# Sparse experts in fp32: from one expert at a time with split weights to four at once in four column tiles of TensorE

## What is computed

```python
lg = xt @ w_rg + b_rg;  g_sel = argmax(lg)                       # one of 4 groups
le = logits of the 8 experts of that group;  e_loc = top 2
gates = p_group * softmax(le_top)
hid = silu(xb @ w_gate[e]) * (xb @ w_up[e])                      # [rows, 512]
y   = hid @ w_down[e]                                            # [rows, 1024]
out[token] += gate * y
```

## Time and profile before

| | |
|---|---|
| median of three runs | 1968.96 us (1967.96 to 1968.97) |
| the profiled execution's own time | 1966.37 us |
| its span, first to last instruction | 1964.6 us |
| mean granted TensorE clock | 0.979 |
| busy: TensorE, its weight loads, VectorE, ScalarE | 94%, 82%, 69%, 56% |
| read from HBM | 406.22 MB, 207 GB/s over the span |
| expert units | 129 of 1536 KB |

### The profile page before, as it was taken

The page is one execution under the profiler, slowest core; times in us unless marked ns, Lnnn a source line. Parts: engine busy times, 40 slices in busy tenths (PEclk is TensorE's granted clock), DMA queues, the critical chain, the costliest instruction groups (busy, mean ns, idle before and its releaser), DMA issues.

```text
span 1964.6 us, 29402 instructions
## 1 busy us (share of the span) xinstructions
PE 1854.7 (94%) x11922; PEld 1601.3 (82%) x11922; DVE 1354.3 (69%) x1835; ACT 1093.9 (56%) x1613; POOL 10.2 (1%) x12
## 2 busy tenths in 40 slices
PE   7998899999999998999999989998899978899997
PEld 5887677777777776999888889998899967799996
DVE  3625999999999996665533376555778785266564
ACT  3234888888988895444323354445644362344444
POOL 0000000000000000000000000000000020000000
PEclk9999999999999999999999999999899988999999
DMA  6325899999999994544244354543498411554420
GB/s 254 119 80 219 308 362 360 358 374 359 362 369 353 364 369 178 210 178 165 88 138 131 113 216 177 185 171 129 166 116 266 140 45 45 182 195 179 182 105 22
DMA packets 56476, 409.30 MB, mean 208 GB/s; under 512 B 15360, under 2 KB 20992, under 8 KB 22160
## 3 DMA queue, kind: packets, MB, share of 16 engines
q1 hardware_dynamic: 51792, 400.51, 57.0%
q10 hardware_dynamic: 4544, 6.85, 1.2%
HBM read 406.22 MB, written 1.11 MB: 207 GB/s over the span
## 4 chain that ended last, share of the span: by engine, by line
PE 67%; DVE 28%; ACT 3%; issue 1%; DMA 0%; DVEq 0%; ACTq 0%; SPq 0%
PE wk L1595 25%; DVE ws_moe L1069 16%; PE acc L1573 11%; PE wk L378 5%; PE wk L1023 3%; PE wk L1948 3%; PE wk L384 2%; PE wk L1763 2%; PE wk L947 2%; PE acc L913 2%; PE acc L730 1%; DVE rstd L305 1%; PE acc L1977 1%; DVE sq L1136 1%; DVE xp_moe L1091 1%
## 5 line engine op out<-in xcount | busy, mean ns | idle before, releaser
L1069 DVE TENSOR_TENSOR ws_moe<-ring,ws_moe 128x1024 fp32r<-128x1024 f32 x384 | 447.5, 1214 | 5.6 <-ACT ws_moe L1062 5.4
L1062 ACT ACTIVATE ws_moe<-ring 128x1024 fp32r<-128x1024 f32 x384 | 384.3, 1051 | 5.1 <-PE wk L1023 2.2
L1595 PE MATMUL wk<-hx,gu 128*128 128x256 f32 x2112 | 276.5, 289 | 5.3 <-DVE hx L1623 4.5
L1595 PEld LDWEIGHTS wk<-hx,gu 128*128 128x128 f32 x2112 | 267.6, 195 | 14.1 <-DVE hx L1623 6.7
L1023 PE MATMUL wk<-ws_moe,xp_moe 128*128 128x512 f32 x1024 | 269.9, 406 | 1.6 <-DVE xp_moe L1091 1.6
L1595 PEld LDWEIGHTS wk<-hx,gu_ffn 128*128 128x128 f32 x2112 | 259.0, 192 | 3.1
L1595 PE MATMUL wk<-hx,gu_ffn 128*128 128x256 f32 x2112 | 260.3, 283 | 0.0
L1573 PE MATMUL acc<-dn_ffn,hh_ffn 128*128 128x512 f32 x1056 | 255.5, 391 | 0.0
L1539 ACT ACTIVATE hT<-hT 128x256 f32<-128x256 f32 x88 | 36.8, 418 | 349.8 <-DVE hT L1642 349.8
L1023 PEld LDWEIGHTS wk<-ws_moe,xp_moe 128*128 128x128 f32 x1024 | 187.9, 189 | 44.2 <-issue 2.8
L1573 PEld LDWEIGHTS acc<-dn_ffn,hh_ffn 128*128 128x128 f32 x1056 | 192.9, 188 | 36.8
(11 more groups left out here) (368 smaller groups left out, 2337.7 us busy)
## 6 DMA issues: line engine op xcount, KB each, us to landing
ring<-in_u_moe SPq DMA_DIRECT2D x129, 1536.0 KB, 8.5
ring<-in_u_ffn SPq DMA_DIRECT2D x88, 1536.0 KB, 6.2
ring<-in_u_qkv SPq DMA_DIRECT2D x12, 1024.0 KB, 5.1
ring<-in_u_ple SPq DMA_DIRECT2D x8, 1280.0 KB, 5.5
ring<-in_u_in SPq DMA_DIRECT2D x9, 1024.0 KB, 5.0
ring<-in_u_glu SPq DMA_DIRECT2D x8, 1024.0 KB, 5.0
ring<-in_u_out SPq DMA_DIRECT2D x4, 1024.0 KB, 4.9
ring<-in_u_o SPq DMA_DIRECT2D x4, 1024.0 KB, 5.1
```

What stands on the lines that cost most here:

```text
L1062: e.activation(WS[:, n % NWS, 0, :], piece(x), ACT.Copy).then_inc(s.m_hi, 1)
L1069: e.tensor_tensor(WS[:, n % NWS, 1, :], piece(x), WS[:, n % NWS, 0, :].bitcast(F32), SUB).then_inc(s.m_lo, 1)
L1595: m = e.matmul(b[:, a * T:(a + 1) * T], gu_of(c, f)[:, x, a * 1024 + k * 128:a * 1024 + (k + 1) * 128], HX[:, y, k, :], start=k == 0 and a ...
```

## The change

- `CAP` goes from 64 to 32 and the experts are worked four at a time (`EPG` = 4, `NG` = 8 groups). Each of the four has its own 32 of the 128 columns of TensorE: its 32 gathered tokens are the stationary operand (128 x 32), its weights stream past in 512 columns, and its result goes to partitions 32x to 32x + 31 of the same PSUM bank.
- The weights are taken in plain fp32 from where they landed. `split_hi`, `split_lo`, `WS`, `tail`, `fold_pe`, `hid_hi`, `hid_lo`, `y_tail` and `y_add` are gone. An expert is no longer worked in halves.
- The DMA units are laid out anew, 128 of 1536 KB, a group being 16 units of three 128 x 1024 pieces; the four experts' pieces of the same rows stand next to each other. They go through eleven slots: six new ones (`ext`) in the space that the split weights had, and the five of `ring`. A slot is free when TensorE has used its third piece (`m_used`).
- The first six units go to `ext` when the mixer's scratch is no longer used (`acc_full` of its last products), the next five when the mixer's last units in `ring` are gone.
- Gather, gates and combine are done once per group of four, 8 times rather than 16.

The core of the diff (places that change with it in the fallback and the host's layout are left out):

```diff
@@ -17,11 +17,12 @@
 NSLOT = 5
-NWS = 8
+NXS = 6
 SCR = 25900
 UNIT = 3072
 NEXP = 32
-CAP = 64
+CAP = 32
+EPG = 4
...
+NG = NEXP // EPG
+NPIECE = 12 * EPG
+NM = NEXP * 12 // 3
+NMS = NXS + NSLOT
...
-        scr2, WS, Xp, MH, gtail, shift, scr2b = area(
...
+        scr2, ext = area("_moe", ("scr", [128, 8192], F32), ("ext", [128, NXS, UNIT], F32))
...
+        def piece_in(e, g, P):
+
+            m = g * NPIECE // 3 + P // 3
+            if P % 3 == 0:
+                e.wait_ge(m_landed[m % NMS], 16 * (m // NMS + 1))
+            return berth_of(m)[:, P % 3 * 1024:P % 3 * 1024 + 1024]
+
+        def moe_sp(e):
+            for m in range(NM):
+                if m < NXS:
+                    e.wait_ge(s.acc_full, fulls("gla") + 1)
+                elif m < NMS:
+                    for w in gone[moe_at - NSLOT + m - NXS]:
+                        e.wait_ge(*w)
+                else:
+                    e.wait_ge(s.m_used, m - NMS + 1)
+                e.dma_start(berth_of(m), A["u_moe"][m]).then_inc(m_landed[m % NMS], 16)
...
+        def gate_up_pe(e, g, k):
+            w = [piece_in(e, g, EPG * k + x) for x in range(EPG)]
+            for a in range(2):
+                for x in range(EPG):
+                    m = e.matmul(wkt[a][slots(x), :], XG[g % 2][:, k, slots(x)], w[x][:, a * 512:a * 512 + 512], start=k == 0, stop=k == 7)
+                    if a and (EPG * k + x) % 3 == 2:
+                        m.then_inc(s.m_used, 1)
+            if k == 7:
+                m.then_inc(s.m_gu, 1)
...
+        def down_pe(e, g):
+            e.wait_ge(s.m_hid, g + 1)
+            e.wait_ge(s.m_G, g + 1)
+            if g + 1 < NG:
+                e.wait_ge(s.m_xa, g + 2)
+                e.wait_ge(s.m_xb, g + 2)
+            for t in range(4):
+                w = [piece_in(e, g, EPG * (8 + t) + x) for x in range(EPG)]
                 for hf in range(2):
-                    for z in range(2):
-                        m = e.matmul(wkt[2 + hf][:, :], MH[:, u % 2, t, :], w[:, z, hf * 512:(hf + 1) * 512],
-                                     start=u % 2 == 0 and t == 0 and z == 0, stop=u % 2 == 1 and t == 1 and z == 1, skip_group_check=True)
-                m.then_inc(s.m_used, 1)
+                    for x in range(EPG):
+                        m = e.matmul(wkt[2 + hf][slots(x), :], mhid[:, t * 128 + CAP * x:t * 128 + CAP * x + CAP], w[x][:, hf * 512:hf * 512 + 512],
+                                     start=t == 0, stop=t == 3)
+                        if hf and (EPG * (8 + t) + x) % 3 == 2:
+                            m.then_inc(s.m_used, 1)
...
+            for g in range(NG):
+                for k in range(8):
+                    gate_up_pe(e, g, k)
+                    if k == 1 and g:
+                        combine_pe(e, g - 1)
+                    if k == 2:
+                        gates_pe(e, g)
+                    if k == 3 and g + 1 < NG:
+                        gather_pe(e, g + 1, 0, wkt[3])
+                    if k == 5 and g + 1 < NG:
+                        e.wait_ge(s.m_G, g + 1)
+                        gather_pe(e, g + 1, 1, wkt[2])
+                hid_pe(e, g)
+                down_pe(e, g)
+            combine_pe(e, NG - 1)
...
         def moe_act(e):
-            split_hi(e, *parts[0:3])
...
+            for g in range(NG):
+                if g + 1 < NG:
+                    gather_act(e, g + 1, wkt[3])
+                e.wait_ge(s.m_gu, g + 1)
+                e.activation(msil, wkt[0][:, :], ACT.Silu).then_inc(s.m_sil, 1)
+                e.wait_ge(s.m_tr, g + 1)
+                e.activation(mhid, wkt[0][:, :], ACT.Copy).then_inc(s.m_hid, 1)
+                e.wait_ge(s.m_used, NPIECE // 3 * (g + 1))
+                if g >= 2:
+                    e.wait_ge(s.m_comb, g - 1)
+                e.activation(ysm[g % 2][:, 512:1024], wkt[3][:, :], ACT.Copy).then_inc(s.m_yl, 1)
...
+                if moe_at <= n < moe_at + NSLOT:
+
+                    e.wait_ge(s.m_used, max(m for m in range(NM) if m % NMS == NXS + (i - moe_at) % NSLOT) + 1)
+                elif n >= NSLOT:
```

More of the change, by code:

```diff
@@ L203, in program @@
         landed = [sem(f"landed{i}") for i in range(NSLOT)]
-        b_landed = [sem(f"b_landed{i}") for i in range(NSLOT)]
+        m_landed = [sem(f"m_landed{i}") for i in range(NMS)]
         ld_bt = [sem(f"ld_bt{i}") for i in range(2)]
@@ L843, in program @@
         rc = S2.get(2)
-        Sel = [S2.get(2, 2, 64) for _ in range(2)]
+        Sel = [S2.get(2, EPG, CAP) for _ in range(2)]
         SG = [S2.get(2, 128) for _ in range(2)]
-        GT_ = [S2b.get(T) for _ in range(2)]
+        XG = [S2.get(8, 128) for _ in range(2)]
+        msil = S2.get(512)
+        mhid = S2.get(512)
+        norms.then("ffn")
+        GT_ = [rstd[:, 1 - norms("ffn") % 2, x * T:(x + 1) * T] for x in range(2)]
         ysm = [sq[:, 4 * x:4 * x + 4, :].rearrange("p a t -> p (a t)") for x in range(2)]
-        msil = [S2b.get(T) for _ in range(2)]
         gm, goh, gex, gsum = R[:, :, 0:1], R[:, :, 1:5], R[:, :, 5:9], R[:, :, 9:10]
@@ L859, in program, with berth_of, gather_pe @@
         first_banks = [i for i in range(4) if i != rank_bank][1:]
[L864 to L894, removed]
+        moe_at = len(units)
+        def berth_of(m):
+            i = m % NMS
+            return ext[:, i, :] if i < NXS else ring[:, (i - NXS + moe_at) % NSLOT, :]
+        def piece_in(e, g, P):
[13 more added lines that the diff above has]
+                e.dma_start(berth_of(m), A["u_moe"][m]).then_inc(m_landed[m % NMS], 16)
+        def gather_pe(e, g, hf, b):
+            e.wait_ge(s.sel, g + 1)
             for k in range(4):
@@ L905, in gates_pe @@
             m.then_inc(s.m_gt, 1)
[L907 to L934, removed]
-            m.then_inc(s.m_tr, 1)
@@ L937, in down_pe, with combine_pe @@
-        def down_pe(e, u):
-            e.wait_ge(s.m_mhl, u + 1)
-            if u % 2 == 0 and u:
-                e.wait_ge(s.m_y, u)
-            for t in range(2):
-                x = (u + 1, 4 + t)
-                e.wait_ge(*split_of(x))
-                w = WS[:, part_at[x] % NWS, :, :]
-                for hf in range(2):
-                    for z in range(2):
-                        m = e.matmul(wkt[2 + hf][:, :], MH[:, u % 2, t, :], w[:, z, hf * 512:(hf + 1) * 512],
-                                     start=u % 2 == 0 and t == 0 and z == 0, stop=u % 2 == 1 and t == 1 and z == 1, skip_group_check=True)
-                m.then_inc(s.m_used, 1)
+        def combine_pe(e, g):
+            e.wait_ge(s.m_y, g + 1)
+            e.wait_ge(s.m_yl, g + 1)
+            if g == 0:
+                acc_in(e, "moe")
+            for d in range(8):
+                m = e.matmul(acc_tile(d), ysm[g % 2][:, d * 128:(d + 1) * 128], GT_[g % 2], start=g == 0 and d % 2 == 0, stop=g == NG - 1,
+                             skip_group_check=True)
+                if g == NG - 1 and d in (1, 3, 5):
+                    m.then_inc(s.m_last, 1)
+            m.then_inc(s.m_comb, 1)
@@ new lines, in slots @@
+        def slots(x):
+            return slice(CAP * x, CAP * x + CAP)
+        def gate_up_pe(e, g, k):
[7 more added lines that the diff above has]
+                m.then_inc(s.m_gu, 1)
@@ L1124, in y_tail @@
[L1124 to L1136 removed]
+            e.wait_ge(s.m_xa, 1)
@@ L1146, in moe_act @@
             gained(1)
-            split_hi(e, *parts[3:5])
             root(e, "ffn")
@@ L1338, in b_out, with b_tile @@
             return wkt[k % 4]
-        def b_tile(n):
-            return ring[:, (n + branch_at) % NSLOT, 0:UNIT]
-        def b_arrived(e, n):
-            e.wait_ge(b_landed[(n + branch_at) % NSLOT], 16 * (n // NSLOT + 1))
-        branch_at = len(units)
+        def b_tile(i):
+            return ring[:, i // 3, i % 3 * 1024:i % 3 * 1024 + 1024]
         def late_sp(e):
@@ L1512, in ffn_act @@
             if c == 0:
-                used(e, NH - 1, 3)
                 ffn_early_act(e, 0)
```

316 lines of the change are left out of this document (86 added, 230 removed).

## The result

| | before | change |
|---|---|---|
| median | 1968.46 us (1965.97 to 1968.97, 4 runs) | 1855.36 us (1853.96 to 1857.44, 4 runs) |
| ratio | | 0.9429, 95% interval 0.9412 to 0.9445 |
| profiled execution: own time, span | 1966.37, 1964.6 us | 1855.12, 1853.3 us |
| expert stage ends (last addition to xT) | 760.85 us | 646.52 us |
| behind the stage, to the end of the span | 1203.75 us | 1206.8 us |

A forecast was written before the change was run, and what follows sets the result against it. VectorE was taken to pace the expert stage; with its splits gone, DMA binds: stream from 201, 440 us for 117 units, then a tail, stage end about 650 against 760.85, 111 us less, 1858 us; range 1845 to 1912.

The forecast's parts named there:

- VectorE paced the old stage: Expert stage before: VectorE's splits set the pace, 34.81 us a pair of experts, holding the weights to 361 GB/s.
- Four tiles at once: Expert matmuls: four column tiles run together, factor 3.8, 0.228 us each, 33.7 us per group at full clock.
- slower-side rival: L925 and L947: tiles run one by one, 0.866 us a matmul, 95 us a group, 2172 us; chance 0.06.
- The stream: Expert weights' DMA becomes the bound at 418 GB/s: 3.76 us a unit, 60.2 a group, 440 for 117 units.
- Units ahead of the stage: Before the experts: eleven units stand ready instead of five, the first six free to go at 138.2 us.
- The start: After the gather: first expert matmul at 197.6 us against 198.36, first slot free 2 us later, stream from 201.
- The stage's end: Expert stage: last unit lands at 641, then last matmuls, copies, combine and addition; ends at 649.3 against 760.85 us.
- TensorE's clock: Expert stage: a pausing TensorE stays at clock 0.50, 64.7 us a group; half expected, 1878 us; chance 0.15.
- Behind the stage unchanged: From the first FFN on: 1203.75 us left alone, its first unit landing at 645, needed at about 650.
- The sum: Whole kernel: the stage ends 111 us earlier, taking the median from 1968.96 to 1858 us.

The follow-up runs named there:

- experiment 5: The kernel before, loading only 1536 of 3072 columns of each expert unit from the sixth on: 1968.1 us (before, beside it: 1968.25).
- experiment 4: The changed kernel, loading only 1536 of 3072 columns of each expert unit from the twelfth on: 1668.01 us.
- experiment 2: The changed kernel without column tiles, each expert matmul taking all 128 gathered columns on the whole array: 2150.06 us.
- experiment 1: The changed kernel with only the five slots of ring, the six of ext taken away: 1876.28 us.
- experiment 3: The changed kernel with gate and up (and the two halves of down) one after the other on the same column tile: 1855.65 us.

## Why the prediction was right

- **VectorE paced the old stage.** Right, and since shown from the other side (experiment 5): at half the bytes the pair still takes 34.8 us.
- **Four tiles at once.** I took 3.8 from the SSM and 0.228 us a matmul; it is 4.0 and 0.215. The group is 32.4 us where I had 33.7 (experiment 4). Neither mattered, since the stream hides both. The slower-side rival's place and price were right as well: without the tiles (experiment 2) the kernel takes 2150 us, 92.7 us a group (L934 of two groups in a row at 351.97 and 444.64 us); the rival had 2172 and 95.
- **The stream.** I took 418 GB/s from the stretches at a full share, 60.2 us a group; it is 425, so 3.70 us a unit and 59.2 a group. Over 117 units 433 us rather than 440: this term was mis-sized by 7 us. That the upper end of the windows was the true rate, and not a burst's, was the choice on which most rested, and no row of before held such a rate for more than 18 us; the windows of 360 had been VectorE's pace (experiment 5).
- **Units ahead of the stage.** Eleven stand ready, six of them issued from 139.75 us on, and the DMA engines are idle (share 0.01 from 190 to 200 us) until the first slot comes free. The prediction did not price the six by themselves; experiment 1 puts them at 21 us.
- **The start** was forecast at 197.6 us for the first expert matmul, and came at 199.16. The gather itself began 1.5 us later than in the trace of before, and the mixer's last matmuls were already as late (138.94 for 137.44 us), ahead of any expert work. I did not follow that shift further. The first slot came free 1.96 us after that matmul (SP's issue at 201.12), where I had 2; the 1.5 us from there to the first bytes had no row behind it, and was about 1 (DMA share 0.00 from 201 to 202 us, 1.07 from 202 to 203).
- **The stage's end** was forecast at 649.3 and came at 646.52: 7 us less stream, against the later start and a slower first window (392 GB/s). The chain behind the last landing, 638.99 to 646.52, took 7.5 us; the forecast's terms, without the landing, were 8.0.
- **TensorE's clock** (rival, 1878). It fell, to 0.75 to 0.90 in windows between 300 and 640 us, as the rival had it, but TensorE kept enough of it: 19.60 to 25.56 us busy of 35, under the stream. The rival had overstated the case by doubling every group. From 299 to 335 us, where I read single bursts, the slow ones (6.54 us for 3.64) stand behind a wait of TensorE, and the stream's rate stayed at 425 or 426 GB/s through all of it.
- **Behind the stage unchanged.** This step failed, by 3.0 us (1206.8 for 1203.75): the prediction had looked at whether the FFN's weights would come late, and not at what else uses the DMA engines. A fuller queue of weights delays the instruction fetch behind the branch (2.43 and 2.93 us of gap became 5.53 and 5.76).
- **The sum.** For the profiled execution it gave 1966.37 - 111 = 1855.4 us, and that execution took 1855.12: the stage ended 3.5 us before the 650 of the sum, and 3.0 us were lost behind it, so two misses cancelled: that the sum came out within 0.3 us is luck, that it came out near is not. The median was forecast from the kernel before's, which lies 2.6 us above its profiled execution; the change's lies 0.2 above its own (1855.36). That offset is the 2.6 us by which 1858 was too high.

## What to carry to other kernels

Before you call a stream bound by memory, ask who frees its slots: here 360 GB/s at a share of 0.93 was VectorE's pace, halving the bytes showed it, and the same queue gave 425 once TensorE freed the slots faster than they filled. Once the stream is the bound, more slots buy no rate, only what lands before the stage begins, so price them by units times unit time. And when a change fills the DMA queue earlier, look at every place where an engine branches over much code: its next instructions may have to come through the same DMA engines.

## What the runs showed of the hardware

- One busy core drew 424 to 426 GB/s through its 16 DMA engines for 400 us on end in the change (235 to 640 us), and the same with five slots (experiment 1) and with another order of the matmuls (experiment 3) in every window read between 300 and 635 us.
- Plain fp32 matmuls of 32 columns of output on four column tiles run four at once: 0.215 us each for 512 columns at full clock, against 0.859 on the whole array, with the moving operands read from slots beside a DMA stream at full rate. Two matmuls in a row on the same tile cost nothing more.
- An engine that branches over a large piece of code stands still for 2.4 to 2.9 us with quiet DMA engines and for 5.5 to 6.5 with full ones (2.6 to 2.9 again once the weights are held back); packets of kind "instruction" move in these gaps, and later in them when the engines are full. Without the branch ScalarE's gap of this kind is 0.17 us and VectorE has none.
- The granted clock of a TensorE that waits for landings between bursts fell to 0.75 to 0.93 in windows of 35 us, and to the lower level in single bursts (6.54 us for 3.64), while the stream's rate, which set the stage's end, stayed the same.
